# Routing of the tokens: the fold's channel sums, the tokens' low parts, the norm factor and the offsets in other places

## The reference

```python
h = modulate(rmsnorm(x, norm_ffn[i]), sh_f, sc_f)        # x * inv_rms * gain * (1 + scale) + shift
g_logits = h @ w_gr + b_gr                               # 4 groups
e_logits = h @ w_er + b_er                               # 32 experts
g_sel = argmax(g_logits); top_val, top_idx = top_k(e_logits of that group, 2)
gate = softmax(g_logits)[g_sel] * softmax(top_val)
act = silu(h @ w_gate[e]) * (h @ w_up[e]) * combine      # per expert, width 256
x = x + g_f * sum_e(act @ w_down[e])
```

## Time and profile before

| | |
|---|---|
| median of 3 runs | 718.63 us (716.36 to 720.48) |
| profiled execution, its own time | 713.47 us |
| its span (first to last instruction) | 711.1 us |
| PE busy | 638.1 us (90%) |
| DVE busy | 364.8 us (51%) |
| ACT busy | 173.1 us (24%) |
| POOL busy | 25.0 us (4%) |
| read from HBM | 268.16 MB, 379 GB/s over the span |

### The profile page before, as it was taken

How to read it: one execution, slowest core, us unless ns; L and a number is a source line. 1 busy time by engine, 2 the same in 40 slices (tenths; PEclk the granted TensorE clock), 3 DMA queues, 4 the chain that set the end, 5 groups by cost and what they waited for, 6 DMA issues and landing times.

```text
span 711.1 us, 11383 instructions
## 1 busy us (share of the span) xinstructions
PE 638.1 (90%) x4266; PEld 381.1 (54%) x4266; DVE 364.8 (51%) x892; ACT 173.1 (24%) x368; POOL 25.0 (4%) x54
## 2 busy tenths in 40 slices
PE   2699999999999999899988999898999898989994
PEld 1487667466655555455454457664445554545542
DVE  1259875988445345333443487744343344333445
ACT  2103343032413113211122133231122112211123
POOL 5100400000000000000000000000000000000000
PEclk9999999999999999999999999999999999999998
DMA  8999973999699999999999999999899899999991
GB/s 329 347 404 393 347 276 134 408 419 412 226 415 420 355 427 386 421 424 420 423 422 423 413 398 410 421 382 401 321 423 421 348 422 423 424 420 420 424 406 59
DMA packets 49694, 269.61 MB, mean 379 GB/s; under 512 B 3813, under 2 KB 5925, under 8 KB 25089
## 3 DMA queue, kind: packets, MB, share of 16 engines
q1 hardware_dynamic: 48880, 268.22, 93.7%
q0 software_dynamic: 784, 1.00, 0.5%
HBM read 268.16 MB, written 1.05 MB: 379 GB/s over the span
## 4 chain that ended last, share of the span: by engine, by line
PE 56%; DMA 32%; DVE 5%; SPq 4%; issue 1%; ACT 1%; POOL 0%; POOLq 0%; ACTq 0%; DVEq 0%
DMA ring<-in_w_up 21%; PE bank L933 12%; PE bank L912 10%; DMA dn_w<-in_w_down 8%; PE bank L900 6%; PE bank L947 5%; PE bank L788 4%; PE bank L637 4%; DMA early_w<-in_w_in 3%; PE bank L865 2%; PE bank L712 2%; PE bank L722 2%; PE bank L563 2%; PE bank L677 1%; SPq L319 1%
## 5 line engine op out<-in xcount | busy, mean ns | idle before, releaser
L912 PE MATMUL bank<-ring,arena 128*64 128x256 f32 x1024 | 116.9, 381 | 17.3 <-DMA ring<-in_w_up 17.3
L900 PE MATMUL bank<-ring,arena 128*64 128x256 f32 x1024 | 118.0, 382 | 6.4 <-DMA ring<-in_w_gate 6.4
L933 PE MATMUL bank<-dn_w,hT 128*64 128x512 f32 x464 | 107.6, 606 | 10.8 <-DMA dn_w<-in_w_down 10.7
L1218 ACT CAST xn_parts<-arena 128x512 fp32r<-128x512 f32 x64 | 39.6, 618 | 303.4 <-DVE arena L1688 303.4
L912 PEld LDWEIGHTS bank<-ring,arena 128*64 128x64 f32 x1024 | 71.9, 137 | 59.2 <-DMA ring<-in_w_up 24.6
L900 PEld LDWEIGHTS bank<-ring,arena 128*64 128x64 f32 x1024 | 76.9, 137 | 39.5 <-issue 12.5
L1663 DVE SCALAR_TENSOR_TENSOR hT<-hT,bank 128x256 f32<-128x256 f32 x32 | 19.8, 620 | 106.4 <-PE bank L912 106.4
L933 PEld LDWEIGHTS bank<-dn_w,hT 128*64 128x64 f32 x464 | 31.5, 138 | 71.9 <-issue 67.4
L947 PE MATMUL bank<-xn_parts,sel 128*128 128x512 f32 x256 | 67.0, 405 | 0.0
L1688 DVE SCALAR_TENSOR_TENSOR arena<-bank,hT,gates 128x512 f32<-128x512 f32 x64 | 48.0, 749 | 35.5 <-PE bank L933 35.5
L947 PEld LDWEIGHTS bank<-xn_parts,sel 128*128 128x128 f32 x256 | 45.7, 188 | 20.9 <-issue 12.4
(11 more groups left out here) (292 smaller groups left out, 684.7 us busy)
## 6 DMA issues: line engine op xcount, KB each, us to landing
ring<-in_w_gate SPq DMA_DIRECT2D x32, 2048.0 KB, 13.9
ring<-in_w_up SPq DMA_DIRECT2D x32, 2048.0 KB, 17.3
dn_w<-in_w_down SPq DMA_DIRECT2D x29, 2048.0 KB, 10.3
ring<-in_w_mod SPq DMA_DIRECT2D x19, 2048.0 KB, 19.3
arena<-in_w_mod SPq DMA_DIRECT2D x4, 2048.0 KB, 17.1
ring<-in_w_in SPq DMA_DIRECT2D x2, 2048.0 KB, 22.7
ring<-in_w_down SPq DMA_DIRECT2D x2, 2048.0 KB, 15.0
early_w<-in_w_in SPq DMA_DIRECT2D x1, 2048.0 KB, 21.3
```

The costliest lines, as they stand in the source:

```text
L900: ins = pe.matmul(bank[2][h * WIN:(h + 1) * WIN, 0:FE], xw[:, b, h, k, :], w[:, h, 0, k, :], start=(k == 0), stop=(k == KT - 1))
L912: ins = pe.matmul(bank[3][h * WIN:(h + 1) * WIN, 0:FE], xw[:, b, h, k, :], w[:, h, 1, k, :], start=(k == 0), stop=(k == KT - 1))
L933: ins = pe.matmul(bank[n][h * WIN:(h + 1) * WIN, :], actT[:, t, h * WIN:(h + 1) * WIN], w[h][:, t, n * HALF:(n + 1) * HALF], start=(t == 0 ...
L1218: act.copy(xn_parts[:, 0, b, at], y_s[:, b, at]).then_inc(e["y_hi"], 1)
```

## The change

- `fold`: VectorE multiplies the shift column into `wroute` and adds up the 8 channel blocks (`fold_shift`, 288 elements per partition), and TensorE sums over partitions with one matmul against `ones`. In layer 0 `fold_shift` stands ahead of the last residual, in layer 1 behind `shift_column`.
- The low parts go from VectorE to GpSimd (`low_parts` there). For them ScalarE writes the normed tokens a second time, unrounded, into `normal`.
- ScalarE takes the last square behind its four turned copies, and VectorE's `mean_square` stands behind its four. In layer 0 VectorE's last accumulate is cut in two halves, one on each side of the choice of experts.
- The offsets that places need come first; those for the windows, and the counts, go to bank 6 in three matmuls of their own behind them. `twice` is gone. The rows of the chosen slots and gates swap banks 6 and 7.
- Both rows of `norm_out_row` are formed in layer 1.

```diff
+            def low_parts(l):
+                for t in range(TT):
+                    pool.wait_ge(S["xn_part1"], TT * l + t + 1)
+                    pool.tensor_tensor(xn_parts[:, 1, t], normal[:, t], xn_parts[:, 0, t].bitcast(F32), ALU.subtract
+                                       ).then_inc(S["xn_part2"], 1)
...
-                    for k in channels:
-                        ins = pe.matmul(bank[(0, 7)[l]][:, 0:RCOLS], ab[:, l, 3, k:k + 1].to_broadcast([P, P]), wroute[:, l, k, :],
-                                        start=(k == 0), stop=(k == KT - 1))
+                    pe.wait_ge(S["ab_ready"], 3 * l + 3)
+                    pe.matmul(bank[(0, 7)[l]][:, 0:RCOLS], ones[:], folded, start=True, stop=True).then_inc(S["fold_done"], 1)
...
-                    norm_out_row(1, bank[5])
+                    norm_out_row(0, bank[4]), norm_out_row(1, bank[5])
...
-                pe.matmul(twice, ones[:], a0.unsqueeze(1).to_broadcast([P, 2, NE]), start=False, stop=False)
-                pe.matmul(twice, ones[:], a1.unsqueeze(1).to_broadcast([P, 2, NE]), start=False, stop=False)
                 pe.wait_ge(S["tot_ready"], l + 1)
...
+                pe.matmul(b[:, 0:2 * NE].rearrange("p (r e) -> p r e", r=2), tot[0:NE, :],
+                          before[0:NE, 0:NE].unsqueeze(1).to_broadcast([NE, 2, NE]), start=False, stop=True).then_inc(S["off_done"], 1)
+                pe.matmul(bank[6][:, 0:NE], tot[0:NE, :], before[0:NE, 0:NE], start=True, stop=True)
+                pe.matmul(bank[6][:, NE:2 * NE], ones[:], a0, start=True, stop=False)
+                pe.matmul(bank[6][:, NE:2 * NE], ones[:], a1, start=False, stop=True).then_inc(S["off_done"], 1)
...
-                squares(2 * l + 1)
+                squares(2 * l + 1, (0,)), squares(2 * l + 1, (1,), (0,))
                 modulated(2 * l + 1, l, 2, hT, shifted=False)
+                squares(2 * l + 1, (1,), (1,))
...
-                    act.activation(xn_parts[:, 0, t], x_res[:, t, :], ACT.Identity, scale=stat[:, 4 + t:5 + t]
+                    act.activation(xn_parts[:, 0, t], x_res[:, t, :], ACT.Identity, scale=stat[:, 4 + t:5 + t])
+                    act.activation(normal[:, t], x_res[:, t, :], ACT.Identity, scale=stat[:, 4 + t:5 + t]
                                    ).then_inc(S["xn_part1"], 1)
...
+            def fold_shift(l):
+
+                done(tt(fold_parts, wroute[:, l], ab[:, l, 3, :].unsqueeze(2).to_broadcast([P, KT, RCOLS]), ALU.mult))
+                dve.tensor_reduce(folded, fold_parts.rearrange("p k r -> p r k"), AX, ALU.add).then_inc(S["ab_ready"], 1)
...
+                modulated(2 * l + 1, l, 2, hT, shifted=False)
                 mean_square(2 * l + 1)
-                modulated(2 * l + 1, l, 2, hT, shifted=False)
-                if l == 1:
+                if l == 0:
+                    accumulate((0, 5), 1, (2,)), accumulate((0, 5), 1, (3,), slice(0, HALF))
...
-                low_parts(0)
-                if l == 0:
-                    accumulate((0, 5), 1, (2, 3))
...
-                low_parts(1)
+                if l == 0:
+                    accumulate((0, 5), 1, (3,), slice(HALF, D))
```

More of the change, by code:

```diff
@@ L819, in route @@
                     pe.wait_ge(S["col_kept"], columns.index((0, 3)) - 1)
-                    fold(range(3)), turn_raw(l, (1,)), fold(range(3, KT))
+                    fold(), turn_raw(l, (1,))
                 else:
@@ L837, in route @@
                 b, a0, a1 = bank[7], asg[:, 0, :], asg[:, 1, :]
-                twice = b[:, 2 * NE:4 * NE].rearrange("p (r e) -> p r e", r=2)
                 pe.matmul(bank[6][0:NE, P:2 * P], a0, ones[:], start=True, stop=False)
@@ L876, in route @@
                 for k in range(4, KT):
-                    if k == 4:
-                        pe.wait_ge(*((S["row_kept"], 1), (S["mod_split"], 2 * split.index((1, 5)) + 1))[l])
-                    else:
+                    if k == 4 and l == 1:
+                        pe.wait_ge(S["mod_split"], 2 * split.index((1, 5)) + 1)
+                    elif k > 4:
                         pe.wait_ge(S["xg_dve" if k % 2 else "xg_act"], 4 * l + (k - 4) // 2 + 1)
@@ L1035, in keep_column, with squares @@
                 act.copy(blocks(stage_of(vec), vec), by_block(bank[banks_of(vec)[0]][:, 0:KT * 32], vec)).then_inc(S["col_kept"], 1)
-            def squares(n):
-                for half in range(2):
-                    for t in range(TT):
+            def squares(n, halves=range(2), tiles=range(TT)):
+                for half in halves:
+                    for t in tiles:
                         if n == 0:
@@ L1154, in keep_row @@
             def keep_row(half, source):
-                act.wait_ge(S["row_done"], 1 + 2 * half)
+                act.wait_ge(S["row_done"], 2 + half)
                 act.copy(gates[:, 0, half * HALF:(half + 1) * HALF], source[:, :]).then_inc(S["row_kept"], 1)
@@ L1184, in route @@
                 act.wait_ge(S["rows_turned"], 2 * l + 1)
[L1185 removed]
+                act.activation(flat(by_token[:, 0:2, :]), bank[7][:, :], ACT.Identity, bias=ones[:, 0:1]).then_inc(S["rows_act"], 1)
             def experts(l):
@@ L1335, in modulated, with accumulate @@
                     ins.then_inc(S["hT_dve"], 1)
-            def accumulate(vec, part, steps=range(KT // 2)):
+            def accumulate(vec, part, steps=range(KT // 2), at=slice(0, D)):
                 acc, r = vec_sum[vec], BIAS_ROW[vec]
@@ L1345, in accumulate @@
                     k = part * (KT // 2) + kk
-                    w = mod_at(place[key])[:, kk, :]
+                    w = mod_at(place[key])[:, kk, at]
                     if kk == 0 and part == 1 and halves(vec)[0] in by_pe:
@@ L1349, in accumulate @@
                     else:
-                        ins = stt(acc, w, cs[:, 2, k:k + 1], acc, ALU.mult, ALU.add)
-                    if kk < KT // 2 - 1:
+                        ins = stt(acc[:, at], w, cs[:, 2, k:k + 1], acc[:, at], ALU.mult, ALU.add)
+                    if kk < KT // 2 - 1 or at.stop < D:
                         done(ins)
@@ L1518, in _ @@
             scale_shift(1, 0, 2)
+            fold_shift(0)
             residual(0, 3, 7, hflat, S["chunk_done"], wo[1])
@@ L1599, in route @@
                     stt(sel[:, t, :], slot_no[:], s1, pick[:, t, :], ALU.is_equal, ALU.add).then_inc(S["sel_ready"], 1)
-                done(dve.tensor_copy(counts, bank[7][:, 3 * NE:4 * NE]))
-                tt(off, bank[7][:, 2 * NE:3 * NE], counts, ALU.subtract)
+                dve.wait_ge(S["off_done"], 2 * l + 2)
+                dve.tensor_copy(off, bank[6][:, 0:NE])
+                done(dve.tensor_copy(counts, bank[6][:, NE:2 * NE]))
                 done(dve.tensor_reduce(cnt, counts, AX, ALU.max))
```

46 lines of the change are left out of this document (20 added, 26 removed).

## The result

The changed kernel takes 721.09 us (median of 20 runs, 716.79 to 725.96), the kernel before 716.88 us (20 runs, 713.03 to 720.48). The ratio is 1.0059, 95% interval 1.0037 to 1.0080: some 4.2 us slower, and more than nothing. The profiled execution took 718.46 us with a span of 716.7; before it was 713.47 with a span of 711.1, so +5.0 in its time and +5.6 in its span.

The account below looks back on a forecast made before the run. Routing was taken to bound the kernel: layer 0's holds up the loads, layer 1's has 2.3 us of DMA slack. -2.47 - 1.27 + 3.7 + 2.2 = +2.2 us on a median of 718.63 gave 720.8, range 714.3 to 724.6.

Parts of the forecast that it names:

- GpSimd blocks VectorE: GpSimd's subtractions hold VectorE's two-SBUF-input instructions in the choice: 3.7 us lost in layer 0, 2.2 in layer 1.
- D: Duration of one GpSimd subtraction of 1024 elements with two SBUF inputs, taken as 2.1 us.
- The sum without GpSimd: All other effects of the change on both layers' routing: -2.47 us in layer 0, -1.27 in layer 1.
- The fold's term: Layer 1's fold as one matmul of about 0.25 us instead of 1.80: -1.55 us.
- VectorE comes later than the logits, so this earns nothing: Layer 0: 10 fold matmuls fewer ready the logits sooner, but VectorE finishes after them: no gain from that.
- -2.05: Layer 0, VectorE ahead of the choice: fold plus bias at 160.05 instead of 162.11 us.
- Layer 1's -1.27: Layer 1's routing without GpSimd: fold -1.55, counting -0.47, three new matmuls ahead of the half vector +0.75 us.
- The second norm row in layer 1: Some 1.1 us more on TensorE ahead of the vector's first half, still done in time: no cost.
- Rival 1: VectorE isn't blocked, or GpSimd's reads slip in between: -3.7 us, time 714.9; chance 0.27.
- rival 2: Half blocked: GpSimd holds the port only while moving data, or D is 1.6; sum about 0, 718.6 us; chance 0.13.
- Rival 3: GpSimd needs much longer, D = 3, and VectorE is blocked: +5.8 us, time 724.4, deciding from D = 2.45; chance 0.15.
- Rival 4: The path isn't where assumed: with layer 1's DMA full anyway its -1.27 is worth 0; no chance of its own given.

Follow-up runs that it names:

- run 4: The changed kernel with layer 0's one fold matmul issued six times into the same place; ratio to before 1.0053.
- run 3: The changed kernel with GpSimd writing zeros twice per low part instead of subtracting, so the gather lacks the low parts; ratio to before 0.9908.
- run 9: The changed kernel with GpSimd's subtraction replaced by a one-input multiply by zero, so the gather lacks the low parts; ratio to before 0.9950.
- run 5: The kernel before with only the fold changed: VectorE forms channel sums, TensorE makes one matmul; ratio to before 0.9957.
- run 7: The changed kernel with low parts on VectorE, in layer 0 behind the table of choices and both sels; ratio to before 0.9915.
- run 8: run 7 with layer 0's one fold matmul issued six times; ratio to the kernel before 0.9941.
- run 10: run 8 with the first norm row made in layer 0 again, ahead of the count; ratio to the kernel before 0.9961.
- run 12: run 11 with layer 0's fold matmul issued six times; ratio to the kernel before 0.9956.
- run 6: The kernel before with only the offsets made first, two wide matmuls gone from the count and three small ones behind; ratio to before 1.0018.
- run 2: The kernel before with only the low parts moved to GpSimd's subtraction, ScalarE making four passes; ratio to before 1.0026.
- run 1: The changed kernel with the low parts back on VectorE and ScalarE making two passes again; ratio to before 0.9951.
- run 11: The kernel before with the one-matmul fold and, in layer 0, the low parts behind the choice; ratio to before 0.9950.

## Why the prediction was right, and where it wasn't

**GpSimd blocks VectorE: right.** D was 2.34 for 2.1; with it the forecast's sum would have been +3.2. Over the choice's free length the block took 3.17 us in layer 0 (3.7 forecast) and 2.33 in layer 1 (2.2 forecast); in run 4, where the choice began when the forecast had it, 3.75. Runs 3 and 9 show that it is the reading. On the Trainium skill's rule (SBUF — State Buffer, "Who interferes with whom"), that a VectorE instruction with two SBUF inputs contends with a GpSimd read, and that the ports they share are an exclusive lock, held for the whole instruction: for two inputs the trace agrees (VectorE held until the end of each 2.34), for one input run 9 does not (1.1 of 2.77). The forecast's own evidence was of another kind than it said: L1294 of the earlier trace rows has one SBUF input (1024 elements in 0.73 us, where the accumulate takes 1.28), while the reduction L1537, with one input too, was not held. So "one input" alone does not say that two instructions can stand side by side, and no run looks at L1294's kind beside a GpSimd that was first.

**The sum without GpSimd, -2.47 and -1.27.** Run 3 shows -2.33 and -1.35. In layer 0 the terms are those of the forecast: VectorE's sum 2.10 earlier behind the last residual (2.05 forecast), 0.26 of it lost in waiting for the logits, and 0.48 in the counting (0.47). In layer 1 the number is right and its terms are not, as said under run 3. The fold's term itself is right: in run 5, where nothing else is changed, the counting begins 1.57 earlier.

**"VectorE comes later than the logits, so this earns nothing", and with it -2.05: failed.** VectorE's fold sum stood at 159.94, where it was forecast (160.05). But the step took the logits' 3.74 us as given; from their start at 156.00 they would have ended at 159.74. They ended at 162.41, since TensorE ran at 1.2 GHz:

```profile
154.00:156.00 2.00, 1.16 (x9) 0.97 (x8) 0.86 (x3) 0.52 (x2) 0.00 (x0) 1.00 1.02 426
156.00:158.00 2.00, 1.94 (x14) 1.82 (x13) 1.91 (x7) 1.66 (x5) 0.00 (x0) 0.82 1.00 418
158.00:166.00 8.00, 8.00 (x57) 6.04 (x60) 5.48 (x8) 4.26 (x4) 5.70 (x3) 0.50 1.01 422
```

Before, TensorE was busy 1.90 of the 2 us from 154 on and the granted clock was 1.00 until 160; the 14 fold passes that went were what it had to do. Run 4 puts work back and has 1.00 from 156 to 164. When the fall comes varies between executions: with the one matmul the logits took from 4.34 (run 3) to 6.56 (run 7), with six 3.94 to 4.38 (runs 4, 8, 10, 12), and with all 16 passes 3.74 (before and run 6) but 5.07 in run 2. So the missing passes make long logits the rule, and are not their only cause. From the last residual's start to VectorE's sum with the logits it was 9.06 us, 8.84 before: +0.22 for -2.05. Run 4 shows that the clock in the logits was not all: with the logits in time the block took more of the choice and the count fell to 1.2 GHz instead, and R0 was no shorter.

**Layer 1's -1.27: failed by the clock.** VectorE's sum came 1.26 sooner behind the turning (1.55 forecast). The choice took 2.33 more (2.2 forecast). From the counting to the half vector it was +0.70 instead of +0.28, since the three extra matmuls cost 1.37 (0.75 forecast), and from the half vector to the gather +1.13 where nothing was forecast: the half vector took 3.64 for 3.27 (by the timeline; the chain, which leaves out what overlaps, has 3.57 and 3.20) and the turned slots 1.91 for 1.16. The forecast had the clock in its range only as ±1.3 from the half vector. The better end of it is what runs 1, 3 and 7 show, without an idle stretch ahead of the counting (1.92 us). The change kept that stretch, because of the block, and so kept the slow half vector of before, with three more matmuls in the slow part.

In the profiled execution R0 is +2.89 for the forecast's +1.23, and R1 +2.90 for +0.93. Their sum, 5.8 for 2.2, is the difference of the spans, 5.6, to 0.2. The medians differ by 4.2 (2.7 to 5.7), so that the forecast of the time is nearer than its parts were.

**Small terms.** The counting in layer 0: -0.47, exact. The second norm row in layer 1, "nothing": right in the change, where TensorE waited for the blocked choice anyway, but not in runs 3 and 7, where it was made at 1.2 GHz and the counting waited for TensorE. The three matmuls in layer 0 and the late down load cost nothing, as said; from the gather to the first gate load it is 12.05 us both before and after. ScalarE's passes started at 159.71, not 158.84, since GpSimd's power took 1.67 instead of 0.69: it stood beside VectorE's accumulates. That late start moved GpSimd's work from 161.1 to 161.97, into a choice that was late as well.

**Rivals.** Rival 1 (not blocked) would have been 714.9, -3.7; run 3 has -6.6 with an interval of -9.2 to -4.0, and run 9 is in effect rival 2, half blocked, but gained 0.5% where it was priced at no change. Rival 3 needed D of 2.45 and over; D was 2.34. Rival 4 is not shown: the fold's -1.55 in layer 1 counted (run 5, -3.1 us with an interval of -4.9 to -1.2), the change's loss there did too (+2.90 of a span longer by 5.6), and for gains beyond it run 10 leaves the matter open.

## What to carry to other kernels

Work given to GpSimd is free only if VectorE has no instruction with two SBUF inputs to run beside it: look at what VectorE does in that stretch, not at GpSimd's idle time. A write cost VectorE nothing here, a one-input pass less than a two-input one. When a change takes work from TensorE or makes it wait, take the next stretch at 1.2 GHz as one end of the range: an off-path engine that gets less to do can become the path. And compare terms, not sums: in layer 1 of run 3 the forecast's number came out of other terms. Measure the parts apart; here one of them gave a gain of 0.4% that the other turned into a loss.

## What the runs showed of the hardware that was not expected

- The order decides who waits. A VectorE accumulate in progress delays GpSimd: in layer 0 its power over 2 elements took 1.66 or 1.67 us for 0.69 in all kernels where the accumulates stood beside it. The accumulates took 2.07 us for one and a half, no longer than elsewhere (2.60 for two).
- GpSimd's tensor_scalar over 1024 elements (2.77 us) is longer than its two-input tensor_tensor (2.34), and holds VectorE for less of it (1.1 us).
- In layer 1 TensorE's clock fell in one of two places. In before, the change and runs 4, 5, 8, 9 and 12 TensorE stood idle for 0.99 us (run 9) to 4.19 us (run 4) ahead of the counting, and the half vector behind it took 3.2 to 3.6 us. In runs 1, 2, 3, 6, 7, 10 and 11 it stood idle for 0.85 us at most, or not at all, and the half vector took 1.92; there the norm rows, or the fold, ahead of it were slow instead. In the change and in run 9 both were. The early fall came without any idle time: in run 2 TensorE was busy for all of 434 to 442 us, and its granted clock was 0.50 from 442 to 446. One trace of each kernel does not show what decides between the two.
- The time of one kernel goes with the mean granted clock of its execution: of the 20 runs of the change, the one at 0.981 took 716.79 us and the one at 0.967 725.96. Half of a per cent between kernels is read from medians of many runs, never from one trace.
